# A routed-expert loop: float32r terms in the combine, and gate/up matrices loaded as one transfer each

## What is computed

```
comb = (for each token: 8 of 64 experts, weighted)
h = silu(einsum('td,edf->tef', t, w_gate)) * einsum('td,edf->tef', t, w_up)
routed = einsum('tef,efd->td', h * comb[..., None], w_down)
shared = (silu(t @ ws_gate) * (t @ ws_up)) @ ws_down
f = routed + shared
x = layer_norm(ALPHA * x + f, ln2_g, ln2_b)
```

## Time and profile before

| | |
|---|---|
| median of the runs | 829.55 us (828.78 to 829.80) |
| span of the profiled execution, first to last instruction | 827.2 us |
| TensorE busy | 811.8 us, 98% of the span |
| VectorE, ScalarE, GpSimd busy | 505.5, 195.3, 92.9 us |
| bytes moved by DMA | 262.03 MB, mean 317 GB/s |
| loop over the expert pairs | from 343.6 us to about 811 us |

### The profile page before, as it was taken

How to read it: one execution, slowest core, us unless ns; L and a number is a source line. 1 busy time by engine, 2 the same in 40 slices (tenths; PEclk the granted TensorE clock), 3 DMA queues, 4 the chain that set the end, 5 groups by cost and what they waited for, 6 DMA issues and landing times.

```text
span 827.2 us, 12702 instructions
## 1 busy us (share of the span) xinstructions
PE 811.8 (98%) x4523; PEld 510.3 (62%) x4523; DVE 505.5 (61%) x1210; ACT 195.3 (24%) x300; POOL 92.9 (11%) x105
## 2 busy tenths in 40 slices
PE   8999999999999999899999999999999999999994
PEld 7876788888788888544545454454545444455552
DVE  6989899999741367535555454545545454454566
ACT  2210112111221005332222223222222322222225
POOL 1119700000010002100000000000000000000021
PEclk9999999999999999999999999999999999999998
DMA  9433344446489946699999999999999999999981
GB/s 333 149 128 103 123 138 147 153 153 115 153 332 419 406 157 272 217 392 418 420 418 418 421 421 421 421 419 420 422 418 421 421 419 422 419 419 420 419 333 52
DMA packets 50548, 262.03 MB, mean 317 GB/s; under 512 B 10504, under 2 KB 11272, under 8 KB 25296
## 3 DMA queue, kind: packets, MB, share of 16 engines
q1 hardware_dynamic: 45904, 252.88, 77.4%
q0 software_dynamic: 4608, 8.66, 2.8%
HBM read 267.10 MB, written 2.53 MB: 326 GB/s over the span
## 4 chain that ended last, share of the span: by engine, by line
PE 97%; DVE 1%; DMA 1%; ACT 1%; issue 0%; SPq 0%; ACTq 0%; DVEq 0%
PE banks L1209 35%; PE banks L1408 27%; PE banks L1448 14%; PE banks L1381 10%; PE banks L1356 3%; PE banks L1310 1%; PE banks L1224 1%; PE banks L1236 1%; PE banks L1386 1%; PE banks L1423 1%; DMA ring<-w_front 1%; PE banks L1474 0%; ACT cgb L685 0%; PE banks L1316 0%; DVE cgb L1119 0%
## 5 line engine op out<-in xcount | busy, mean ns | idle before, releaser
L1408 PE MATMUL banks<-high,low 128*64 128x512 f32 x848 | 225.6, 592 | 0.1
L1209 PE MATMUL banks<-xT,ring 128*128 128x264 f32 x768 | 176.3, 389 | 0.7 <-DMA ring<-w_front 0.7
L1209 PEld LDWEIGHTS banks<-xT,ring 128*128 128x128 f32 x768 | 144.5, 190 | 30.9 <-issue 5.5
L1408 PEld LDWEIGHTS banks<-high,low 128*64 128x64 f32 x848 | 73.7, 137 | 143.8 <-issue 142.7
L1119 DVE TENSOR_TENSOR cgb<-cgb,banks 128x264 f32<-128x264 f32 x248 | 90.0, 423 | 51.8 <-PE banks L1381 51.8
L1164 DVE SCALAR_TENSOR_TENSOR high<-banks,sml,low 128x1024 f32<-128x1024 f32 x31 | 39.8, 1284 | 122.3 <-ACT low L673 122.3
L1381 PEld LDWEIGHTS banks<-xT,low 128*128 128x128 bf16 x744 | 70.3, 98 | 35.4 <-issue 24.3
L1381 PE MATMUL banks<-xT,low 128*128 128x264 bf16 x744 | 90.2, 276 | 0.0
L518 POOL DMA_INDIRECT low<-x_rows_dram,idx x32 | 31.9, 997 | 427.6 <-DVE idx L1064 406.8
L1408 PE MATMUL banks<-ring,low 128*64 128x512 f32 x176 | 77.5, 593 | 0.0
L1448 PE MATMUL banks<-high,mu 128*64 128x512 f32 x336 | 76.7, 598 | 0.3 <-DVE cgb L1119 0.3
(11 more groups left out here) (295 smaller groups left out, 924.3 us busy)
## 6 DMA issues: line engine op xcount, KB each, us to landing
high<-w_gu SPq DMA_DIRECT2D x108, 1024.0 KB, 24.5
high<-w_dn SPq DMA_DIRECT2D x42, 1024.0 KB, 23.9
ring<-w_front SPq DMA_DIRECT2D x78, 512.0 KB, 3.3
ring<-w_gu SPq DMA_DIRECT2D x22, 1024.0 KB, 25.6
us<-w_dn SPq DMA_DIRECT2D x11, 1024.0 KB, 24.2
bgb<-w_dn SPq DMA_DIRECT2D x6, 1024.0 KB, 22.1
xcb<-w_dn SPq DMA_DIRECT2D x5, 1024.0 KB, 22.3
xT<-x_t SPq DMA_DIRECT2D x4, 264.0 KB, 3.7
```

The lines of the kernel that those rows point to most:

```text
L1209: ins = pe.matmul(psum[:, 6 + n % 2, 0:T], ring[:, n % RING, k], rhs[:, k], start=(k == 0), stop=(k == KC - 1))
L1408: ins = pe.matmul(psum[SL * j:SL * j + SL, GU_BANK, :], xg[:, k, SL * j:SL * j + SL], gu[slots[j]][:, k], start=(k == 0), stop=(k == KC - 1))
```

## The change

Two edits. In the combine, `y_terms` (three bfloat16 terms) becomes `y_pair`: two terms of type float32r, a 4-byte type that TensorE multiplies at reduced precision. `sw` becomes float32r too, in a place of its own. ScalarE's second term and VectorE's third fall away, with their two semaphores. In the loop, each gate/up matrix is loaded by one transfer (128 rows of 16384 bytes) once the whole slot is free, and TensorE waits for both whole matrices before the first gate/up matmul; `gu_mid` is gone. The loads before the loop still come in halves, on the one semaphore of the slot. VectorE waits for the stores of the token rows (`rows_stored`) before the loop, since `y_pair` lies where two of these rows were.

```
-        y_terms, = carve(y_flat.bitcast(BF16)[:, 0:3 * D], (3, D))
+        y_pair = nc.alloc_sbuf_tensor_at("y_pair", [P, 2, D], F32R, offset=low_end - 4 * 2 * D)
+        sw = nc.alloc_sbuf_tensor_at("sw", [P, 2, T], F32R, offset=high_end - 4 * (KC * 2 * F + 64 + D))
@@ refill, SyncE
-                    for h, through in enumerate((gu_mid, gu_done)):
-                        sp.wait_ge(through, it + 1)
-                        for s, e in zip(slots, experts):
-                            sp.dma_start(gu[s][:, HC * h:HC * h + HC], w_gu[bass.ds(e, 1), :, HC * 2 * F * h:HC * 2 * F * (h + 1)].rearrange("o p f -> (o p) f")).then_inc(gu_in[s][h], 16)
+                    sp.wait_ge(gu_done, it + 1)
+                    for s, e in zip(slots, experts):
+                        sp.dma_start(gu[s], w_gu[bass.ds(e, 1)].rearrange("o p f -> (o p) f")).then_inc(gu_in[s], 16)
@@ visit, ScalarE
-                    act.activation(y_terms[:, 0], psum[:, 4:6].rearrange("p b f -> p (b f)"), ACT.Copy, scale=gain[:, u]).then_inc(first_term, 1)
-                    act.wait_ge(rest_ready, it + 1)
-                    act.activation(y_terms[:, 1], y_rest, ACT.Copy).then_inc(second_term, 1)
+                    act.activation(y_pair[:, 0], psum[:, 4:6].rearrange("p b f -> p (b f)"), ACT.Copy, scale=gain[:, u]).then_inc(first_term, 1)
@@ before the loop, VectorE
+                dve.wait_ge(rows_stored, 16 * TC)
@@ visit, VectorE
-                    dve.scalar_tensor_tensor(y_rest, psum[:, 4:6].rearrange("p b f -> p (b f)"), gain[:, u], y_terms[:, 0], ALU.mult, ALU.subtract).then_inc(rest_ready, 1)
-                    dve.wait_ge(rest_ready, it + 1)
-                    dve.wait_ge(second_term, it + 1)
-                    dve.tensor_tensor(y_terms[:, 2], y_rest, y_terms[:, 1], ALU.subtract).then_inc(y_split, 1)
+                    dve.scalar_tensor_tensor(y_pair[:, 1], psum[:, 4:6].rearrange("p b f -> p (b f)"), gain[:, u], y_pair[:, 0], ALU.mult, ALU.subtract).then_inc(y_split, 1)
@@ combine_chunk, TensorE
-                    for term in range(3):
-                        ins = pe.matmul(psum[:, bank, 0:T], y_terms[:, term, n * P:n * P + P], sw[:, u], start=(term == 0 and not shared), stop=(term == 2))
+                    for term in range(2):
+                        ins = pe.matmul(psum[:, bank, 0:T], y_pair[:, term, n * P:n * P + P], sw[:, u], start=(term == 0 and not shared), stop=(term == 1))
@@ visit, TensorE
-                            if k % HC == 0:
-                                pe.wait_ge(gu_in[slots[j]][k // HC], loaded + (16 if slots[j] == 3 else 0))
+                            if k == 0:
+                                pe.wait_ge(gu_in[slots[j]], loaded + 16 + (16 * 2 if slots[j] == 3 else 0))
-                        if k == HC - 1:
-                            ins.then_inc(gu_mid, 1)
```

More of the change, by code:

```diff
@@ L13 @@
 BF16 = mybir.dt.bfloat16
+F32R = mybir.dt.float32r
 P = 128
@@ L140, in build @@
         low = sb("low", [P, 6 * D])
+        low_end = nc.sbuf_base
         high = sb("high", [P, 2 * NT * T + 4096 + 2 * NT * SEG + NT * ROW + 2 * NT * 32 + 2 * NT * NS])
+        high_end = nc.sbuf_base
         b_in_sm, bb, bT = carve(low[:], (2, NT, 32), (2, NT, 32), (2, KC, P))
@@ L173, in build @@
         dn = [dn_ring[:, i] for i in range(SLOTS)] + [dn_4, dn_5, dn_6, dn_7]
-        val_flat, pos, s_flat, iota, pk_flat, small, group, token_no, sw_flat = carve(
-            xT[:].rearrange("p k t -> p (k t)"), (TC * E * 3,), (TC, E), (2 * TC * SL,), (2, SL), (TC * E // 2,), (64,), (3, TC, RG), (T,), (T,))
+        val_flat, pos, s_flat, iota, pk_flat, small, group, token_no = carve(
+            xT[:].rearrange("p k t -> p (k t)"), (TC * E * 3,), (TC, E), (2 * TC * SL,), (2, SL), (TC * E // 2,), (64,), (3, TC, RG), (T,))
         val, = carve(val_flat.bitcast(BF16), (TC, E, 2, 3))
         S, = carve(s_flat.bitcast(BF16), (2, TC, 2 * SL))
-        sw, = carve(sw_flat.bitcast(BF16), (2, T))
         pk, = carve(pk_flat.bitcast(BF16), (TC, E))
@@ L279, in build @@
         shared_used = sem("shared_used")
-        gu_in = [[sem(f"gu_slot{i}_half{h}_loaded") for h in range(2)] for i in range(6)]
+        gu_in = [sem(f"gu_slot{i}_loaded") for i in range(6)]
         dn_in = [sem(f"dn_slot{i}_loaded") for i in range(8)]
@@ L289, in build @@
         xg_ready = sem("xg_ready")
-        gu_mid = sem("gu_first_half_done")
         gu_done = sem("gu_done")
@@ L296, in build @@
         first_term = sem("first_term_ready")
-        rest_ready = sem("rest_ready")
-        second_term = sem("second_term_ready")
         y_split = sem("y_split")
@@ L381, in load_gu @@
                     for h in halves:
-                        sp.dma_start(gu[s][:, HC * h:HC * h + HC], w[:, HC * 2 * F * h:HC * 2 * F * (h + 1)]).then_inc(gu_in[s][h], 16)
+                        sp.dma_start(gu[s][:, HC * h:HC * h + HC], w[:, HC * 2 * F * h:HC * 2 * F * (h + 1)]).then_inc(gu_in[s], 16)
                 parts = [("gu", 2, 0), ("dn", 2, 0), ("gu", 3, 1), ("dn", 3, 1), ("gu", 0, 4), ("dn", 4, 2), ("gu", 4, 2), ("dn", 5, 3), ("gu", E, 3), ("dn", E, 6)]
@@ L1320, in _ @@
                 turn_scores()
-                for h in range(2):
-                    pe.wait_ge(gu_in[3][h], 16)
+                pe.wait_ge(gu_in[3], 16 * 2)
                 for k in range(KC):
```

## The result

The changed kernel takes 831.14 us (median of 20 runs, 829.93 to 831.85), the kernel before 829.60 us in the runs beside it (828.78 to 831.01). The ratio is 1.0019 (95% interval 1.0012 to 1.0025), so 1.6 us more: a small loss, just inside the 0.2% that the prediction called no change. The predicted time was 829.6 us, with a range of 825.5 to 834.

What follows compares the result with a forecast made beforehand. TensorE's work and the DMA stream were taken to bound the end together, within half a microsecond. Visit 31's start moves by 2.9 + 1.5 - 4.2 = +0.2, the last combine by -0.1: net +0.1, 829.6 us, range 825.5 to 834.

Steps and rivals of the forecast that it cites:

- The end is set by the landing of pair 31, TensorE's savings are hidden: Loop's end: visit 31 starts when its gate/up weights land, 796.6 us; TensorE's shorter path stays hidden behind that.
- TensorE's own path: 789.1: TensorE's work up to visit 31 gets 7.3 us shorter, so it alone could start that visit at 789.1 us.
- The combine gives 0.1 us a visit, float32r costs 0.12 us a matmul: Combine: 16 matmuls instead of 24 at 0.12 us each; VectorE's adds take most of the 0.96 us, leaving 0.1 a visit.
- The rival of 0.23 us a matmul: Combine: each float32r matmul takes 0.23 us, so TensorE binds; about +25 us, 854 us, chance 0.10.
- Whole matrices: +2.9: Start of visit 31: TensorE waits for both whole gate/up matrices, not halves, and starts 2.9 us later.
- Late first refill: +1.5, at most 3.4: Start of the loop: the first refill's first halves are issued 3.44 us later; +1.5 us, bounds 0.5 and 3.4.
- Long rows: -4.2: Gate/up loads: 16384-byte rows save a fixed 9 ns each, 4.2 us by pair 31's landing, bounds -1.2 and -6.0.
- The sum: Whole execution: pair 31's landing and visit 31's start +0.2 us, last combine 0.1 shorter, net +0.1 us.
- The gather: Gathered rows beside longer weight rows: landing in 10 to 11 us, with no wait on TensorE.
- The waits begin at visit 23, about 1 us each: First gate/up step: TensorE waits for weights from about visit 23 on, about 1 us each.
- Long rows that bring more: Weight loads: 13 ns saved per row and 0.5 us for the late start; -2.7 us, 826.9 us, chance 0.22.
- Long rows that bring little: Visit starts from about 23 on: 2.5 ns a row gives +3.1 us, 832.7; no gain gives 833.9; chance 0.18.

Runs made afterwards that it cites:

- the terms alone: Kernel before with the two float32r terms in the combine, its loads still in halves: 829.34 us, ratio 1.0002 to the kernel before.
- lighter loads: Changed kernel with only the first half of each down matrix loaded in the loop, 5 MB a visit: span 820.1 us, one execution.
- the whole wait alone: Kernel before, but TensorE waits for both halves of both gate/up matrices before the first gate/up matmul: 832.58 us, ratio 1.0035 to the kernel before.
- the late issue alone: Kernel before, but the first halves of each refill are issued with the second ones, after all of gate/up: 831.81 us, ratio 1.0031 to the kernel before.
- the version with one term: Changed kernel without the second float32r term in the combine's matmuls (still written): visit period 14.14 us, against 14.26 in the changed kernel.
- the version with short rows: Changed kernel with its waits, but each gate/up matrix in two transfers of 8192-byte rows: 834.99 us, ratio 1.0063 to the kernel before.
- the last pairs in halves: Changed kernel, pairs 26 to 31 loaded in halves and started at the first ones: 829.31 us; with the first two refills in halves too, 826.47 us.
- the first two refills in halves: Changed kernel, pairs 3 and 4 loaded in halves, the first ones at half of gate/up: 829.09 us, ratio 0.9997 to the kernel before.
- the loads alone: Kernel before with the change's whole-matrix refills and waits, its three bfloat16 terms kept: 831.48 us, ratio 1.0025 to the kernel before.

## Why the prediction was right, and where it was off

- *The end is set by the landing of pair 31, TensorE's savings are hidden.* That the stream sets the end and hides the savings is shown: the terms alone leave the time where it was, and with lighter loads TensorE's own path starts visit 31 at 789.3. That it is pair 31 whose landing counts is true of the changed kernel; with the whole wait alone and the late issue alone the time is lost in the pairs up to 25, and nothing waits for pair 31.
- *TensorE's own path: 789.1.* 789.3 was measured, but the agreement is luck: two terms are off and cancel. Up to visit 25 the path got 702.13 - 698.29 = 3.8 us shorter, where 2.4 was forecast, and from there to visit 31 it got 94.26 - 91.01 = 3.2 us shorter, where 4.4 + 0.45 was.
- *The combine gives 0.1 us a visit, float32r costs 0.12 us a matmul.* The visit got 0.15 us shorter. Right in size, but not for the reason given. The prediction has the first chunk ready 0.12 us sooner and VectorE's adds moving with it; they did not move, the first add starts 0.62 us after the combine in both kernels. What was gained is that TensorE, with 24 matmuls, had been 0.19 us behind the last add at the start of down, and with 16 it is 0.05 behind. The first chunk's 0.12 us are real only in the version with one term. The rival of 0.23 us a matmul is out, since 16 of them would take 3.7 us and they take 2.63 with VectorE's pauses.
- *Whole matrices: +2.9.* Measured alone: +2.9 (1.0035, interval 1.9 to 3.9 us), paid in visits 22 to 25.
- *Late first refill: +1.5, at most 3.4.* This is the term that was mis-sized most: alone it is +2.6 (1.0031, 1.6 to 3.6 us), by the windows 2.1. The reasoning was right in kind. The prediction first found 1.9 us, from the landing of the first refill, and then took 0.4 off because the queue had not been full before. The windows show that giving back too, but from 3.1 us at 358 us down to 2.1 at 374, so the 1.9 should have stood. What the time shows above the 2.1 us, 0.5, lies within its interval.
- *Long rows: -4.2.* Measured alone, by the version with short rows: -3.6 by the medians, -4.6 by the start of visit 31 in the profiles.
- *The sum.* 2.9 + 2.6 - 3.6 = +1.9, and the change measured +1.6. The forecast said +0.1. Of the difference the late refill has 1.1 us (0.6 by the windows) and the long rows, by the medians, 0.6. Each of the three terms has an interval of a microsecond or more either way, so that they add up to within 0.3 is more than they can promise.
- *The gather.* Forecast at 10 to 11 us without a wait. It lands after 8.3 to 11.0 us, 10.2 in the median, in the gathers of 400 to 790 us, where it took 8.1 before:

```profile
DMA to landing us min/median/max: 8.3/10.2/11.0
```

- *The waits begin at visit 23, about 1 us each.* They begin at visit 21, up to 1.2 us each. The stream was later than thought and TensorE's visits shorter (14.26 us, not 14.3); how much each did is not shown.
- *The rivals.* Long rows that bring more: no, 424 GB/s as forecast. Long rows that bring little: the direction came out (+1.6), but not by this mechanism; the rows gave what was expected and the late start took it.

Left open is about a microsecond in the versions with the last pairs in halves: alone they gained 1.4 us of 2.5, yet with the first two refills in halves the gain under the changed kernel is 4.4 us by the ratios, and the two apart add up to 1.8 + 1.4 = 3.2. The intervals are as wide as that, the spans of one kernel spread over 2 us, and no run separates the two.

## What to carry to other kernels

When a queue of loads and an engine are both full, count the change on the landing of the last load that something waits for, and price a faster engine at nothing until that landing moves. Look up which load that is: it was pair 31's in the changed kernel, and pair 25's with the whole wait alone. A lead of buffers hides the late issue of a load only once a backlog stands: at the start of a loop, add up what the stream has moved by the time the queue is full in both versions. A gap of 3.1 us was worth 2.1 here, since the other version was short of work a little later, and closing the first gap opened a second one. In this kernel long rows paid in the middle of the long stream, and short transfers at both its ends.

## What the runs showed of the hardware that was not expected

- A float32r matmul of 264 columns follows its like in about 0.12 us as bfloat16 does (in the combine of visit 18 they start at 605.69, 605.81 and 605.94 us), but its 128 x 128 weight load takes twice as long (mean and median, on the weight-load side of TensorE):

```profile
L1375 PEld LDWEIGHTS banks<-sw,y_pair x496: 186/188/193, 363.1 to 807.5; 128*128 128x128 f32 x166
```

The bfloat16 weight load took 98 ns. Between equal matmuls it is hidden. At the head of the group it seems not to be: the second matmul starts 0.23 us after the first (605.46 to 605.69), where with bfloat16 it was 0.12 (608.25 to 608.37). That is where the 0.12 us of the first chunk went; that the weight load is the reason is not shown.

- Rows twice as long beside it delay a gather of 4096-byte rows by 2.1 us, from 8.1 to 10.2. The experiments bear this out: its median is 10.3 with the loads alone and 8.0 with the changed kernel's short rows. From the use of one gather to the issue of the next 2.7 us pass, in both kernels (613.91 - 611.18 in the earlier trace rows, 610.92 - 608.19 now), so a gather has 14.41 - 2.7 = 11.7 us before and 11.5 now. Of the 3.6 us to spare, 1.3 are left.
